# Differential attention heads: one weighted sum of a difference instead of two, with new step lists for the last layer

## The chip, the core and the metric

The kernel runs on one core of a Trainium2 chip. The metric is the device time of one execution in microseconds (us), the median of the runs. Five engines of the core work side by side and meet at semaphores: TensorE (PE; its weight loads are shown apart as PEld), VectorE (DVE), ScalarE (ACT), GpSimd (POOL) and the DMA queue of SyncE (SP). TensorE writes to PSUM alone; its operands come from SBUF.

## What is computed

A token matrix x of 256 x 1024 (float32) goes through four layers: two of one model and two of another. The change touches the fourth, `odd_layer`. Its core, cut to what matters:

```python
cq, ckv, kpe, qd, kd, vd, gate = _split(rmsnorm(x) @ w_in, SPLIT_O)
q  = (rmsnorm(cq) @ w_cq_b)                    # 8 latent heads of 96
kv = (rmsnorm(ckv) @ w_ckv_b)                  # 8 heads: 64 of key, 64 of value
oc = attend_blocks(qc, kc, v_c, 96 ** -0.5)    # 8 latent heads
# 4 differential heads, each with two queries and two keys of 64, one value of 128:
s1 = einsum('bqhd,bkhd->bhqk', q1, k1) * scale
s2 = einsum('bqhd,bkhd->bhqk', q2, k2) * scale
p  = softmax(s1) - lam * softmax(s2)
od = einsum('bhqk,bkhd->bqhd', p, v)
od = rmsnorm(od, g_sub_d) * (1.0 - lam_init)
x  = x + (concat([oc, od]) * silu(gate)) @ w_out
```

`lam` is one scalar, worked out from four small vectors.

## The kernel before

Every projection is a product in three passes: a weight tile and the activations are split into a high part (ACT, L853, `hi`) and a low part (DVE, L1288, `lo`), and PE multiplies high x low, high x high and low x high (L2053 to L2055; the gate's columns at L2130 to L2133). Weights stream through a ring of 8 slots of 128 x 1024; each slot is a **unit** (chunk, number). In the fourth layer chunks 0 to 5 are the projections, 6 and 7 the gate, 8 and 9 the output projection.

Attention is cut into instances of one softmax over 256 x 256, numbered j = 2p + h (pair p, half h). Pairs 0 to 3 are the four differential heads, their two halves being the two softmaxes. Pairs 4 to 7 hold two latent heads each. The steps, with the engine on which each stands:

- `prep k` (PE, L2032) transposes queries and keys, `D k` (ACT or DVE) copies them out of PSUM. prep 0 to 3 are differential, prep 4 to 11 latent heads. Before them stand, on DVE, `RED` (sums of squares), `SCL` (scaling), `GN` (gains), `ROT` (rotation) and `KCAT`, with `SQ` on ACT and `POW` (a power of 16 values, L755) on POOL, for qd, kd (differential) and qc, kc (latent).
- `S p` (PE, L2227) scores of both halves; `X p,h` (DVE, L1437) row maximum; `E p,h` (ACT, L985 and L987) exponential, with the row sum.
- `SC p,h` (DVE, L1594 to L1609) multiplies the exponentials by a factor per row: the reciprocal of the row sum, and in half 1 of a differential pair also by `lam[:, 2:3]`, which holds the negative of lambda (L1606).
- `T p,h` (PE, L2264) transposes the weights into one of two PSUM banks, `C p,h` (ACT, L997) copies them to `probT`.
- `PV p` (PE, L2249) adds up the value products of the pair. For a differential pair both halves add into the same 128 rows of PSUM, so the subtraction happens there.
- `OD` (ACT, L954 and L955) takes the result of a differential pair out. Its normalisation is a chain: `ODSUM` (PE, L2531), `ODMS` (DVE, L1982), `ODP` (POOL, L831), `DG` (DVE, eight instructions, L1987), `OF` (PE, L2539), and `ON` (DVE, L1994), which also needs `ODG` (POOL, L835), the product with the gate. `SILU` (ACT) makes the gate ready.
- `MP`, `MH`, `ML` (DVE, ACT, DVE) split a latent pair's result; `out 0,k` is unit (8,k). `take c` (ACT and DVE) copies a projection's chunk out of PSUM, and `gt` one of the gate.

What sets the order: four lists, `PE_3`, `ACT_3`, `DVE_3` and `POOL_3`, one per engine, each carried out strictly in turn. The PSUM bank for transposed data alternates in the order in which prep and T steps stand in `PE_3` (`FILL`). Weights, DMAs and the other three layers have lists of their own.

Of the kernel before, what the change touches and what calls it, by code (L numbers as in the profile page):

```python
# [8 lines left out]
ALU = mybir.AluOpType  # L9
# [5 lines left out]
T = 256  # L15
NT = T // P
D = 1024
# [115 lines left out]
FILL = {}  # L133
# [139 lines left out]
for _kind, *_at in PE_2:  # L273
    if _kind == "prep":
        number("prep2", _at)
    elif _kind == "T":
        number("attn2", (2 * _at[0] + _at[1],))
PE_3 = [("unit", 1, 0), ("unit", 1, 1), ("unit", 1, 2), ("unit", 1, 3), ("unit", 2, 0), ("F", 0), ("unit", 2, 1),
        ("unit", 2, 2), ("unit", 2, 3), ("F", 1), ("unit", 3, 0), ("unit", 3, 1), ("prep", 0), ("prep", 1),
        ("unit", 4, 0), ("prep", 2), ("unit", 5, 0), ("S", 0), ("unit", 5, 1), ("unit", 5, 2), ("S", 1),  # L280
        ("unit", 5, 3), ("prep", 3), ("T", 0, 0), ("unit", 6, 0), ("unit", 6, 1), ("S", 2), ("T", 0, 1),
# [3 lines left out]
        ("unit", 7, 3), ("prep", 10), ("T", 4, 1), ("ODSUM",), ("prep", 7), ("prep", 11), ("S", 6), ("T", 5, 0),  # L285
        ("PV", 4), ("OF",), ("T", 5, 1), ("S", 7), ("PV", 5), ("out", 0, 0), ("T", 6, 0), ("T", 6, 1), ("out", 0, 1),
        ("T", 7, 0), ("T", 7, 1), ("PV", 6), ("PV", 7), ("out", 0, 2), ("out", 0, 3)]

ACT_3 = [("take", 0), ("LAMX",), ("hi", 2, 0), ("hi", 2, 1), ("hi", 2, 2), ("hi", 2, 3), ("hi", 3, 0), ("hi", 3, 1),
# [11 lines left out]

DVE_3 = [("take", 0), ("LAMD",), ("GT",), ("LS",), ("lo", 2, 0), ("lo", 2, 1), ("lo", 2, 2), ("lo", 2, 3),
         ("lo", 3, 0), ("LAMS",), ("LSC",), ("take", 1), ("lo", 3, 1), ("lo", 4, 0), ("RED", "qd"), ("LL", 0),
         ("lo", 5, 0), ("lo", 5, 1), ("SCL", "qd"), ("take", 2), ("ROT", "qd"), ("RED", "kd"), ("lo", 5, 2),
         ("LL", 1), ("take", 3), ("SCL", "kd"), ("ROT", "kd"), ("take", 4), ("KCAT",), ("RED", "qc"), ("lo", 5, 3),
# [10 lines left out]

POOL_3 = [("POW", "lora"), ("POW", "qd"), ("POW", "kd"), ("POW", "qc"), ("POW", "kc"), ("ODP",), ("ODG",)]


number("norm6", range(4))  # L320
# [32 lines left out]
def net(nc, a, out):  # L353
# [37 lines left out]
    fac = place("fac", [P, 72, 2])  # L391
# [12 lines left out]
    prob = place("prob", [P, 4, 512])  # L404
# [13 lines left out]
    OF = (SUM, 2)  # L418
# [15 lines left out]
    kd = extra[:, 0:2560].rearrange("p (t h c d) -> p t h c d", t=NT, h=10, c=2)  # L434
# [31 lines left out]
    lam = small[:, 296:300]  # L466
# [104 lines left out]
    def instances(stage):  # L571
        out = []
# [25 lines left out]
        if stage == "attn3":  # L598
            for h in range(8):
                out.append(dict(q=pair_row("prep3", "qd", h), k=pair_row("prep3", "kd", h), bias=None,  # L600
                                v=(z3, 1440 + P * (h // 2), P), causal=False, half=0, pair=h // 2,
                                first=h % 2 == 0, last=h % 2 == 1, lam=h % 2 == 1))
            for h in range(8):
                out.append(dict(q=reg[0:MLA_D, BLOCK["prep3"]["qc", h], :], k=reg[0:MLA_D, BLOCK["prep3"]["kc", h], :],
                                bias=None, v=(lo_kv, P * h + HD, HD), causal=False, half=h % 2, pair=4 + h // 2,
                                first=True, last=True))
# [91 lines left out]
    def heads_of(name):  # L698

        return {"qd": heads(z3[:, :, 416:928]), "kd": heads(z3[:, :, 928:1440]), "qc": heads(lo_q, MLA_D), "kc": kcat}[name]  # L700

    def product_of(stage, p):

# [136 lines left out]
    def _(act):  # L840
# [136 lines left out]
        def exponents(stage, j):  # L977

            i, it = INST0[stage] + j, INST[stage][j]
            act.wait_ge(max_ready, i + 1)  # L980
            if it["bias"] is None and j >= 4:
                act.wait_ge(t_filled, FILL[stage, j - 4] + 1)
            w = P if it["causal"] else T
            src, sign = (ps[:, score_bank(i), :], 1.0) if it["bias"] is None else (prob[:, i % 4, :], -1.0)
            n.activation(prob[:, i % 4, 0:w], src[:, 0:w], ACT.Exp, bias=negm[:, i, 0:1], scale=sign,  # L985
                         accum_out=den[:, i, 0:1])
            n.activation(prob[:, i % 4, 256:512], src[:, 256:512], ACT.Exp, bias=negm[:, i, 1:2], scale=sign,  # L987
                         accum_out=den[:, i, 1:2]).then_inc(exp_ready, 1)
# [277 lines left out]
    def _(dve):  # L1266
# [4 lines left out]
        def link(ins):  # L1271

            chain[0] += 1
            ins.then_inc(sem("dve_chain"), 1)
            dve.wait_ge(sem("dve_chain"), chain[0])
# [324 lines left out]
        def scaled(stage, p, h):  # L1600

            if h == 0:
                factors(stage, p)
            k = INST0[stage] + 2 * p + h
            if INST[stage][2 * p + h].get("lam"):
                link(v.tensor_tensor(fac[:, k, :], fac[:, k, :], bc(lam[:, 2:3], [P, 2]), ALU.mult))  # L1606
            w = P if INST[stage][2 * p]["causal"] else T
            v.tensor_scalar(prob[:, k % 4, 0:w], prob[:, k % 4, 0:w], fac[:, k, 0:1], None, ALU.mult)
            v.tensor_scalar(prob[:, k % 4, 256:512], prob[:, k % 4, 256:512], fac[:, k, 1:2], None, ALU.mult)\  # L1609
             .then_inc(probs_ready, 1)  # L1610
# [402 lines left out]
    def _(pe):  # L2013
# [217 lines left out]
        def weighted(stage, j0):  # L2231
# [3 lines left out]
            for j in two:  # L2235
                it, p = inst[j], inst_pair(stage, j)
                if it["opens"] and p >= 2:
                    pe.wait_ge(*bank_taken(p - 2))
            for j in two:
                f = FILL[stage, j]  # L2240
                pe.wait_ge(t_drained[f % 2], f // 2 + 1)
            for kt in range(NT):
                for j in two:
                    i, it, p = i0 + j, inst[j], inst_pair(stage, j)
                    buf, lo, w = it["v"]
                    rows = slice(64 * it["half"], 64 * it["half"] + w)
# [3 lines left out]
                                   start=it["first"] and kt == 0, stop=it["last"] and kt == NT - 1,  # L2250
                                   skip_group_check=True)
                    if kt == NT - 1:
                        ins.then_inc(pv_done, 1)

        def transposed(stage, j):

# [390 lines left out]
```

## Time and profile before

| | |
|---|---|
| median of 3 runs | 919.93 us (919.16 to 924.9) |
| the profiled execution | 921.26 us, of which the span is 919.4 us |
| PE busy | 882.9 us, 96% of the span |
| DVE, ACT, POOL busy | 624.9, 493.8, 79.0 us |
| DMA | 148.71 MB, 162 GB/s mean |
| the fourth layer's step lists | from about 778 us to 905 us |

The 1.86 us between the profiled execution's time and its span lie outside all engines' work. Matmul rows of a timeline overlap by the pipeline, so the cost of a piece on PE is the distance between starts, not the duration of a row.

### The profile page before, as it was taken

The numbers are of one execution on the slowest core, as the hardware profiler recorded it, in microseconds if no ns is written. First come the engines' busy times: TensorE is split into PE (matmuls) and PEld (weight loads), VectorE is DVE, ScalarE is ACT, GpSimd is POOL, SyncE is SP. The second block draws the span as 40 slices with busy tenths as digits, with TensorE's granted clock in tenths as the row PEclk, the third lists the DMA queues.
The fourth block names the chain that finished last, engine by engine and source line by source line (L and its number), as shares of the span: only waits on it lengthen the run. The fifth ranks groups of instructions, "written<-read, shape, count | busy, mean of one in ns | idle before, by whom it ended". The sixth has DMA issues, their size and how long they took to land.

```text
span 919.4 us, 14636 instructions
## 1 busy us (share of the span) xinstructions
PE 882.9 (96%) x5540; PEld 755.7 (82%) x5540; DVE 624.9 (68%) x1139; ACT 493.8 (54%) x913; POOL 79.0 (9%) x88
## 2 busy tenths in 40 slices
PE   4999899999999999999999999998999999989998
PEld 3868578999998878777899999886879868868976
DVE  4788987455564467877655555545588777989873
ACT  4446865454553345666544444434456775565662
POOL 2100000000000000000000000000386000231010
PEclk9999999999999999999999999998999999999999
DMA  9664135655566556433655555664854314745201
GB/s 340 206 209 151 37 98 178 184 184 183 184 224 187 184 172 194 152 124 115 192 162 179 185 183 189 228 190 143 251 166 144 128 38 131 218 136 147 84 24 46
DMA packets 96789, 148.71 MB, mean 162 GB/s; under 512 B 6272, under 2 KB 59680, under 8 KB 96592
## 3 DMA queue, kind: packets, MB, share of 16 engines
q1 hardware_dynamic: 94512, 140.50, 48.6%
q10 hardware_dynamic: 1296, 4.87, 1.6%
q0 software_dynamic: 912, 2.41, 1.0%
q8 instruction: 45, 0.74, 0.3%
q14 instruction: 24, 0.20, 0.1%
HBM read 146.71 MB, written 1.05 MB: 161 GB/s over the span
## 4 chain that ended last, share of the span: by engine, by line
PE 79%; issue 6%; DVE 6%; POOL 4%; ACT 3%; DMA 2%; SPq 0%; POOLq 0%; DVEq 0%; ACTq 0%
PE ps L2053 22%; PE ps L2055 22%; PE ps L2054 21%; PE ps L2227 3%; PE ps L2249 3%; PE ps L2264 2%; POOL small L755 1%; PE ps L2043 1%; DVE w_lo L1288 1%; ACT hA L868 1%; PE ps L2032 1%; DMA w_raw<-in_w_in_e 1%; POOL extra L797 1%; PE ps L2130 1%; PE ps L2133 1%
## 5 line engine op out<-in xcount | busy, mean ns | idle before, releaser
L1288 DVE TENSOR_TENSOR w_lo<-w_raw,w_hi 128x1024 fp32r<-128x1024 f32 (+1 forms) x261 | 310.1, 1207 | 132.5 <-ACT w_hi L853 128.4
L853 ACT ACTIVATE w_hi<-w_raw 128x1024 fp32r<-128x1024 f32 (+1 forms) x261 | 267.2, 1041 | 156.4 <-DMA w_raw<-in_w_gate_up 56.4
L2053 PE MATMUL ps<-w_hi,hT_lo 128*128 128x512 f32 (+3 forms) x448 | 176.9, 395 | 6.6 <-DVE w_lo L1288 4.7
L2053 PE MATMUL ps<-hT_hi,w_lo 128*128 128x256 f32 x640 | 181.4, 283 | 0.0
L2055 PE MATMUL ps<-hT_lo,w_hi 128*128 128x256 f32 x640 | 181.1, 283 | 0.0
L2054 PE MATMUL ps<-hT_hi,w_hi 128*128 128x256 f32 x640 | 181.1, 283 | 0.0
L2055 PE MATMUL ps<-w_lo,hT_hi 128*128 128x512 f32 (+3 forms) x448 | 171.5, 383 | 0.0
L2054 PE MATMUL ps<-w_hi,hT_hi 128*128 128x512 f32 (+3 forms) x448 | 171.4, 383 | 0.0
L2053 PEld LDWEIGHTS ps<-hT_hi,w_lo 128*128 128x128 f32 x640 | 122.9, 192 | 0.4 <-DVE w_lo L1288 0.3
L2054 PEld LDWEIGHTS ps<-hT_hi,w_hi 128*128 128x128 f32 x640 | 122.9, 192 | 0.0
L2055 PEld LDWEIGHTS ps<-hT_lo,w_hi 128*128 128x128 f32 x640 | 122.9, 192 | 0.0
L2053 PEld LDWEIGHTS ps<-w_hi,hT_lo 128*128 128x128 f32 x448 | 85.7, 191 | 29.0 <-issue 7.8
L2055 PEld LDWEIGHTS ps<-w_lo,hT_hi 128*128 128x128 f32 x448 | 85.6, 191 | 16.3
L2054 PEld LDWEIGHTS ps<-w_hi,hT_hi 128*128 128x128 f32 x448 | 85.9, 192 | 14.1
L2053 PE MATMUL ps<-w_hi,hid_lo 128*128 128x512 f32 x176 | 69.5, 395 | 0.0
L2055 PE MATMUL ps<-w_lo,hid_hi 128*128 128x512 f32 x176 | 69.4, 395 | 0.0
L2054 PE MATMUL ps<-w_hi,hid_hi 128*128 128x512 f32 x176 | 69.4, 394 | 0.0
L997 ACT ACTIVATE probT<-ps 128x384 f32<-128x384 f32 (+1 forms) x72 | 37.5, 539 | 31.6 <-PE ps L2264 28.8
L760 POOL TENSOR_TENSOR small<-small 128x1 f32<-128x1 f32 x10 | 5.6, 556 | 482.6 <-DVE small L1295 482.6
L2227 PE MATMUL ps<-reg 64*128 64x256 f32 (+2 forms) x288 | 39.8, 371 | 2.4 <-ACT prob L987 2.2
L2264 PE MATMUL ps<-table,prob 128*128 128x128 f32 x248 | 38.5, 279 | 1.4 <-DVE prob L1609 0.6
L2053 PEld LDWEIGHTS ps<-w_hi,hid_lo 128*128 128x128 f32 x176 | 33.2, 188 | 7.6
(235 smaller groups left out, 1196.8 us busy)
## 6 DMA issues: line engine op xcount, KB each, us to landing
w_raw<-in_w_gate_up SPq DMA_DIRECT2D x176, 256.0 KB, 4.3
w_raw<-in_w_down SPq DMA_DIRECT2D x44, 512.0 KB, 4.3
w_raw<-in_w_in_e SPq DMA_DIRECT2D x38, 512.0 KB, 5.2
w_raw<-in_w_qkv_o SPq DMA_DIRECT2D x24, 512.0 KB, 4.4
w_raw<-in_w_in_o SPq DMA_DIRECT2D x20, 512.0 KB, 3.7
w_raw<-in_w_out_e SPq DMA_DIRECT2D x16, 512.0 KB, 3.5
w_raw<-in_w_out_o SPq DMA_DIRECT2D x16, 512.0 KB, 3.5
w_raw<-in_w_in_e SPq DMA_DIRECT2D x8, 268.0 KB, 4.9
```

The lines of the kernel that those rows point to most:

```text
L755: g.tensor_tensor(o, i, halfs[:, 0:n], ALU.pow).then_inc(sem(name + "_rstd"), 1)
L797: pool.dma_start(bias_na[64 * half:64 * half + 64, :, u, :], src).then_inc(sem("bias_in"), 16)
L853: n.activation(w_hi[:, u % RING, 0:size], w_raw[:, u % RING, 0:size], ACT.Copy).then_inc(hi_ready, 1)
L868: n.activation(hA[:, t, cols], x[:, t, cols], ACT.Square, scale=D ** -0.5, accum_out=ss[:, 2 * t + c:2 * t + c + 1]).then_inc(norm_sem("ss ...
L997: n.activation(probT[:, i % 4, 0:w], ps[:, TB + f % 2, 0:w], ACT.Copy).then_inc(t_drained[f % 2], 1)
L1288: v.tensor_tensor(w_lo[:, u % RING, 0:size], w_raw[:, u % RING, 0:size], w_hi[:, u % RING, 0:size].bitcast(F32), ALU.subtract).then_inc(lo ...
L2053: m.matmul(o, lhs[1], rhs[0], start=start, stop=False)
L2054: m.matmul(o, lhs[0], rhs[0], start=False, stop=False)
L2055: return m.matmul(o, lhs[0], rhs[1], start=False, stop=stop)
L2227: ins = m.matmul(o, it["q"][:, t * P:(t + 1) * P], it["k"][:, 0:w], start=True, stop=True)
L2249: ins = m.matmul(ps[rows, OB + p % 2, cols], buf[:, kt, lo:lo + w], probT[:, i % 4, src], start=it["first"] and kt == 0, stop=it["last"] a ...
L2264: ins = m.transpose(ps[:, TB + f % 2, col:col + P], prob[:, i % 4, 256 * t + kt * P:256 * t + kt * P + P], ident)
```

## The change

The instances of the differential heads get a mark `diff`, and each is now its own sum (`first` and `last` both true). In `SC p,1` of such a pair the two multiplications by the factor give way to two SCALAR_TENSOR_TENSOR instructions: half 1 times its factor, plus the already scaled half 0, in place. Then `T p,1` alone is done (`T p,0` and `C p,0` are gone for p < 4), and `PV p` multiplies that one matrix with the values: two matmuls in the program instead of four. The exponentials of pair p + 2 wait for `T p,1` also where they waited for `T p,0`. All four lists of the fourth layer are replaced.

```diff
-        ("unit", 2, 2), ("unit", 2, 3), ("F", 1), ("unit", 3, 0), ("unit", 3, 1), ("prep", 0), ("prep", 1),
-        ("unit", 4, 0), ("prep", 2), ("unit", 5, 0), ("S", 0), ("unit", 5, 1), ("unit", 5, 2), ("S", 1),
...
+        ("unit", 2, 2), ("unit", 2, 3), ("F", 1), ("unit", 3, 0), ("unit", 3, 1), ("prep", 1), ("unit", 4, 0),
+        ("prep", 0), ("unit", 5, 0), ("prep", 2), ("unit", 5, 1), ("prep", 3), ("S", 0), ("unit", 5, 2),
+        ("unit", 5, 3), ("S", 1), ("T", 0, 1), ("unit", 6, 0), ("PV", 0), ("unit", 6, 1), ("S", 2), ("unit", 6, 2),
...
-                                first=h % 2 == 0, last=h % 2 == 1, lam=h % 2 == 1))
+                                first=True, last=True, lam=h % 2 == 1, diff=True))
...
+    def turned(stage, j):
+
+        return j | 1 if INST[stage][j].get("diff") else j
...
-                act.wait_ge(t_filled, FILL[stage, j - 4] + 1)
+                act.wait_ge(t_filled, FILL[stage, turned(stage, j - 4)] + 1)
...
+            if h and INST[stage][2 * p].get("diff"):
+                dve.wait_ge(probs_ready, k)
+                for t in range(NT):
+                    row = slice(T * t, T * t + T)
+                    ins = v.scalar_tensor_tensor(out=prob[:, k % 4, row], in0=prob[:, k % 4, row],
+                                                 scalar=fac[:, k, t:t + 1], in1=prob[:, (k - 1) % 4, row],
+                                                 op0=ALU.mult, op1=ALU.add)
+                ins.then_inc(probs_ready, 1)
+                return
...
-            for j in two:
+            used = tuple(j for j in two if turned(stage, j) == j)
+            for j in used:
                 f = FILL[stage, j]
                 pe.wait_ge(t_drained[f % 2], f // 2 + 1)
             for kt in range(NT):
-                for j in two:
+                for j in used:
...
-                        ins.then_inc(pv_done, 1)
+                        ins.then_inc(pv_done, 2 // len(used))
```

The first place where the lists put work elsewhere and the prediction speaks of it is PE around the end of the differential heads' normalisation (`ps` is PSUM, `table` the identity or, in the rows L2531 and L2539, the squares and diagonals). PE before, from prep 7 to PV 5:

```order
L2032 MATMUL ps<-table,hA 96x128 x4
L2264 MATMUL ps<-table,prob 128x128 x4
L2531 MATMUL ps<-table 128x1 x8
L2032 MATMUL ps<-table,extra 96x128 x4
L2032 MATMUL ps<-table,hA 96x128 x4
L2227 MATMUL ps<-reg 128x256 x4
L2264 MATMUL ps<-table,prob 128x128 x4
L2249 MATMUL ps<-probT,extra 64x256 x4
L2539 MATMUL ps<-table 128x512 x2
L2264 MATMUL ps<-table,prob 128x128 x4
L2227 MATMUL ps<-reg 128x256 x4
L2249 MATMUL ps<-probT,extra 64x256 x4
```

The same place now (line numbers of the new file):

```order
L2044 MATMUL ps<-table,extra 96x128 x4
L2044 MATMUL ps<-table,hA 96x128 x4
L2544 MATMUL ps<-table 128x1 x8
L2239 MATMUL ps<-reg 128x256 x4
L2277 MATMUL ps<-table,prob 128x128 x8
L2262 MATMUL ps<-probT,extra 64x256 x4
L2552 MATMUL ps<-table 128x512 x2
L2277 MATMUL ps<-table,prob 128x128 x8
L2262 MATMUL ps<-probT,extra 64x256 x4
```

Between ODSUM (128x1) and OF (128x512) stood two preps, S 6, T 5,0 and PV 4; now S 7, T 5,0, T 5,1 and PV 4 stand there.

The second place is DVE between `KCAT` and the first `SC 0,1`. Now, from the end of KCAT (`small` holds the sums, `negm` the maxima, `fac` the factors):

```order
L1291 TENSOR_TENSOR w_lo<-w_raw,w_hi 128x1024 x2
L1748 TENSOR_REDUCE small<-reg 128x16
L1750 TENSOR_SCALAR small<-small 128x16
L1440 TENSOR_REDUCE negm<-ps 128x2 x2
L1756 TENSOR_TENSOR hA<-hA,small 128x2x768
L1597 RECIPROCAL fac<-den 128x4
L1620 TENSOR_SCALAR prob<-prob,fac 128x256
L1621 TENSOR_SCALAR prob<-prob,fac 128x256
L1945 COPY reg<-ps 128x512
L1609 TENSOR_TENSOR fac<-fac,small 128x2
L1614 SCALAR_TENSOR_TENSOR prob<-prob,fac 128x256 x2
```

The rows L1748 and L1750 come twice in turn there (RED kc, then RED qc; shown once). Before, one RED stood ahead of X 0,0 and X 0,1, and no SCL between them and SC 0,0; now two REDs and SCL kc (the row L1756) do.

## Rows read from the trace of the kernel before

**Rows 1.** PE's waits in 797:919.4: engine, line waited for, us in total, times, longest.
```profile
PE ps L2032 <- DVEq L1926: 2.7, 1, 2.7
PE ps L2539 <- DVE table L1987: 1.7, 1, 1.7
PE ps L2032 <- DVE lr_lo L1956: 0.6, 1, 0.6
```
**Rows 2.** Windows: busy PE, PEld, DVE, ACT, POOL; granted clock; DMA share, GB/s.
```profile
820.00:822.00 2.00, 2.00 (x6) 1.58 (x5) 1.85 (x2) 0.00 (x0) 0.00 (x0) 0.50 0.00 0
```
**Rows 3.** PE's timeline at PV 1: start, duration, line, tiles, matmuls.
```profile
848.07 0.60 PE L2264 MATMUL ps<-table,prob 128*128 128x128 f32 x4
848.51 1.89 PE L2249 MATMUL ps<-probT,z 128*128 128x256 f32 x8
850.33 1.14 PE L2227 MATMUL ps<-reg 64*128 64x256 f32 x8
```
**Rows 4.** PE's timeline, 808:824: matmuls of one shape at either clock.
```profile
820.46 0.63 PE L2053 MATMUL ps<-w_hi,hT_lo 128*128 128x512 f32 x1
820.89 0.63 PE L2054 MATMUL ps<-w_hi,hT_hi 128*128 128x512 f32 x1
...
822.17 0.40 PE L2054 MATMUL ps<-w_hi,hT_hi 128*128 128x512 f32 x1
822.40 0.40 PE L2055 MATMUL ps<-w_lo,hT_hi 128*128 128x512 f32 x1
```
**Rows 5.** DVE's timeline: a scaling, then a two-input instruction of the same length.
```profile
844.00 0.35 DVE L1609 TENSOR_SCALAR prob<-prob,fac 128x256 f32<-128x256 f32 x1
...
846.06 0.42 DVE L1380 TENSOR_TENSOR tmp<-extra,table 128x256 f32<-128x256 f32 x1
```
**Rows 6.** DVE's timeline: SCL kd, RED qc, a split, D 1, SCL qc; ODMS.
```profile
813.69 1.23 DVE L1744 TENSOR_TENSOR z<-z,small 128x1024 f32<-128x1024 f32 x1 [1.26 <-POOL small L755]
...
820.40 1.75 DVE L1736 TENSOR_REDUCE small<-reg 128x16 f32<-128x1536 f32 x1
...
825.10 1.22 DVE L1288 TENSOR_TENSOR w_lo<-w_raw,w_hi 128x1024 fp32r<-128x1024 f32 x1
826.23 0.69 DVE L1933 COPY reg<-ps 128x512 f32<-128x512 f32 x1
...
828.29 1.75 DVE L1744 TENSOR_TENSOR extra<-extra,small 128x1536 f32<-128x1536 f32 x1
...
878.94 0.17 DVE L1982 TENSOR_SCALAR small<-ps 128x8 f32<-128x8 f32 x1 [2.11 <-PE ps L2531]
```
**Rows 7.** POOL's timeline: two powers of 16 values, and ODG (L835).
```profile
799.16 2.91 POOL L755 TENSOR_TENSOR small<-small 128x16 f32<-128x16 f32 x1 [9.33 <-DVE small L1738]
...
822.45 3.94 POOL L755 TENSOR_TENSOR small<-small 128x16 f32<-128x16 f32 x1 [8.79 <-DVE small L1738]
...
881.00 2.40 POOL L835 TENSOR_TENSOR z<-z 128x1024 f32<-128x1024 f32 x1
```
**Rows 8.** The chain that ended last, at DG: start, us, what.
```profile
880.89 2.19 DVE table L1987 x2
...
883.40 1.25 DVE table L1987 x6
```
**Rows 9.** PE's timeline: scores of latent heads, and ODSUM.
```profile
861.52 1.89 PE L2227 MATMUL ps<-reg 96*128 96x256 f32 x8
...
876.98 1.92 PE L2531 MATMUL ps<-table 128*128 128x1 f32 x16
```
**Rows 10.** PE's timeline after two earlier idle times.
```profile
637.04 1.70 PE L2043 MATMUL ps<-table,hA 128*128 128x128 f32 x8 [2.46 <-DVE hA L1305]
...
640.38 0.63 PE L2054 MATMUL ps<-w_hi,hT_hi 128*128 128x512 f32 x1
...
738.30 1.13 PE L2227 MATMUL ps<-reg 64*128 64x256 f32 x8 [2.24 <-ACT prob L987]
```
**Rows 11.** Windows again: the stretch around 738.
```profile
720.00:760.00 40.00, 37.34 (x259) 28.80 (x258) 29.86 (x69) 30.80 (x75) 0.00 (x0) 1.00 0.25 77
```

More of the change, by code:

```diff
@@ L278 @@
 PE_3 = [("unit", 1, 0), ("unit", 1, 1), ("unit", 1, 2), ("unit", 1, 3), ("unit", 2, 0), ("F", 0), ("unit", 2, 1),
-        ("unit", 2, 2), ("unit", 2, 3), ("F", 1), ("unit", 3, 0), ("unit", 3, 1), ("prep", 0), ("prep", 1),
-        ("unit", 4, 0), ("prep", 2), ("unit", 5, 0), ("S", 0), ("unit", 5, 1), ("unit", 5, 2), ("S", 1),
-        ("unit", 5, 3), ("prep", 3), ("T", 0, 0), ("unit", 6, 0), ("unit", 6, 1), ("S", 2), ("T", 0, 1),
[3 rows of a table removed]
[L285 to L289, printed above, removed]
[11 rows of a table removed]
[L302 to L305, printed above, removed]
[10 rows of a table removed]
-POOL_3 = [("POW", "lora"), ("POW", "qd"), ("POW", "kd"), ("POW", "qc"), ("POW", "kc"), ("ODP",), ("ODG",)]
+        ("unit", 2, 2), ("unit", 2, 3), ("F", 1), ("unit", 3, 0), ("unit", 3, 1), ("prep", 1), ("unit", 4, 0),
+        ("prep", 0), ("unit", 5, 0), ("prep", 2), ("unit", 5, 1), ("prep", 3), ("S", 0), ("unit", 5, 2),
+        ("unit", 5, 3), ("S", 1), ("T", 0, 1), ("unit", 6, 0), ("PV", 0), ("unit", 6, 1), ("S", 2), ("unit", 6, 2),
+        ("prep", 6), ("unit", 6, 3), ("prep", 4), ("S", 3), ("T", 1, 1), ("prep", 5), ("unit", 7, 0), ("prep", 8),
[4 rows of a table added]
+        ("out", 0, 3)]
+ACT_3 = [("take", 0), ("hi", 2, 0), ("LAMX",), ("hi", 2, 1), ("hi", 2, 2), ("hi", 2, 3), ("hi", 3, 0), ("hi", 3, 1),
[10 rows of a table added]
+DVE_3 = [("GT",), ("take", 0), ("LAMD",), ("lo", 2, 0), ("LS",), ("lo", 2, 1), ("lo", 2, 2), ("LSC",), ("lo", 2, 3),
[13 rows of a table added]
+POOL_3 = [("POW", "lora"), ("POW", "qd"), ("POW", "kd"), ("POW", "kc"), ("POW", "qc"), ("ODP",), ("ODG",)]
 number("norm6", range(4))
```

51 rows, old and new, of tables (ACT_3, DVE_3, PE_3) are left out of this document.

## Prediction

> **What bounds the kernel now.** I read the page first: in the small table above PE is busy for 96% of the span, so matmuls removed count unless PE then waits. The table of PE's waits in the fourth layer comes next [rows 1]: only three are named, 0.64, 2.75 and 1.71 us. They are the opening of prep 1's PSUM bank (DVE had yet to take LL 1, the low part of F 1), prep 2's wait for the rotated keys kd, and OF's wait for DG. Then the windows: behind the 2.75 us the granted clock is 0.50 of full speed, that is 1.2 instead of 2.4 GHz [rows 2], and a matmul of 512 columns starts every 0.43 us instead of every 0.23 [rows 4]. Eight of them ran so, from 818.75 to 822.17: 8 x 0.2 = 1.6 us. What PE lost in this layer is thus 0.64 + 2.75 + 1.6 + 1.71 = **6.7 us**. The timelines of DVE, ACT and POOL are read last, for whether they can keep up: what a step of PE waits for is a date on one of them.
>
> **What goes.** On PE, per differential head, one T and half of PV. T costs 0.44 us and PV 1.82, from start to start [rows 3]. Four heads: 4 x 0.44 + 4 x 0.91 = **5.4 us**, all on an engine with nothing beside it. The matmul records of PV are eight for four instructions, and halve to four. ACT loses four C of 0.5 us each; ACT has idle time before most exponentials, so I cost that at nothing.
>
> **What is added.** DVE: in SC p,1 two TENSOR_SCALAR of 0.35 us become SCALAR_TENSOR_TENSOR with two inputs; no row shows these operands. The nearest is a TENSOR_TENSOR of equal length, 0.42 us [rows 5]. So 8 x 0.07 = 0.6 us over the layer. Below, it could be nothing (0.35); above, a row of twice the length would be 0.7, or 8 x 0.35 = 2.8 us in all. I take 0.42, since length and inputs agree. The Trainium skill speaks against the change here ("VectorE: DVE Perf Modes", Mode 2x_2P): a float32 tensor_scalar may use both read ports for one tensor and make two results a cycle, which an instruction with two tensors can't. By its rate the difference would be an estimated 256 / 0.96 GHz / 2 = 0.13 us each, 1.1 us in all, and by it T 0,1 would come 0.1 us later and the gain be 5.8. The wait for the own earlier SC p,0 is met, since the factor's product stands between.
>
> **Where PE waits now.** I followed the new lists with the durations of before, noting at each step of PE when its producers finish.
>
> 1. Unit 4,0 now follows prep 1, and still needs LL 1 at 811.5: 0.7 us, as before.
> 2. Prep 2 was late because ROT kd was. Between now stand prep 0 and unit 5,0 (2.8 us). But ROT kd moves too: D 1 (0.6) is put ahead of SCL kd, where POOL's power was late anyway (813.69 [rows 6]), so it is hidden; take 4 (1.2) is put ahead of ROT kd, so kd is ready at 818.95 and not 817.7. PE stands at prep 2 at about 818.3. Small waits at the second half of unit 5,0 (DVE's take 4), at prep 2 and at S 0 (D 2, behind SQ kc and a split on ACT) come to 0.4 + 0.7 + 0.4 = 1.5 us, each under a microsecond, and no fall of the clock.
> 3. **T 0,1** is the new late one. DVE before did SCL kd, ROT kd, take 4, KCAT and a first RED from 813.69 to 822.4 (820.40, 1.75 and the small instruction behind it, 2.0 in all [rows 6]). The same five stand there now with two splits among them, each 1.13 from start to start (825.10 to 826.23): RED kc ends at 824.5 to 824.7. POOL then takes 2.9 to 3.9 us for the power [rows 7]; DVE does RED qc (2.0) and both X (1.2) meanwhile, to 827.7. SCL kc takes 1.8, like SCL qc at 828.29 [rows 6]; a drain and the two SC of a pair took 826.23 to 828.29, 2.1 us, and now 0.2 more: SC 0,1 is done at 831.8 to 832.5. PE has S 0 at 823.15, then two units, S 1, and stands at T 0,1 at 831.0. Wait 0.8 to 1.5; I take 1.2. Units 5,2 and 5,3, S 1 and the steps behind have no other cover.
> 4. Up to unit 7,0 DVE runs nearly without a pause; its split for unit 6,3 is ready 0.1 us before it is used and that for 7,0 0.4 us late. 0.4 us.
> 5. **OF.** Count from the end of unit 7,3. DG ends after prep 7 and 11 (0.9), ODSUM (1.8), then ODMS to DG, 878.94 to 880.89 (1.95: POOL's ODP lies between), then DG itself, 880.89 to 884.65 (3.76 [rows 6, 8]): 8.4 us. PE is there after 0.9 + 1.8 + S 7 1.7 + two T 0.8 + PV 4 1.0 = 6.2 us (ODSUM and S by [rows 9] less 0.1 to 0.2 of overlap, prep and T by [rows 3], and a latent PV, whose values are 64 wide, near half of a differential one). Wait **2.2 us**. So OF waits longer than before, though ODSUM now stands later in front of more latent work.
> 6. Behind OF nothing is late: SC 7,0 is done some 0.5 us before T 7,0, ML 7 more than 1 us before out 0,3.
>
> Waits now: 0.7 + 1.5 + 1.2 + 0.4 + 2.2 = **6.0 us**, but no slow clock. The sum is 5.4 + 6.7 - 6.0 = 6.1; a few more switches between kinds of matmuls (0.2) leave **5.9 us**. Against the profiled execution: span 919.4 - 5.9 = 913.5 and time 921.26 - 5.9 = 915.4. That execution was 1.3 us over the median, so the median should be 919.93 - 5.9 = **914.0 us**.
>
> **Why DG is slow, and one rival.** Two of DG's eight instructions take 2.19 us, the other six 1.25 [rows 8], and the first two lie exactly under ODG on POOL, 881.00 to 883.40 [rows 7]. This is what the Trainium skill says ("SBUF — State Buffer", Who interferes with whom): DVE in a 2-port mode and GpSimd exclude each other for a whole instruction. Now SILU, and with it ODG's permission, ends 4.7 us after unit 7,3 by my count, and ODP also at 4.7; DG is free at 4.8. They meet again. If SILU comes over 1.6 us later, DG runs in 8 x 0.21 = 1.7 us and OF waits 0.1 us: gain 5.9 + 2.1 = 8.0, 911.9 us. Chance 14%. With luck at T 0,1 and unit 7,0 as well it passes 9.2.
>
> **The other ways.**
> - The clock falls behind OF's wait. After idle times of 2.24 us it stayed at 1.00 [rows 10, 11]; after 2.46, with a further pause, a matmul took 0.63 us and not 0.40 [rows 10, 4]; here it is 2.2. Cost 1.6 us, as measured in [rows 4]: 915.6 us. Chance 22%.
> - DVE binds longer. From T 0,1 to unit 7,0 the margins are 0.1 to 0.8 us, so each us by which DVE falls behind is PE's. Against it stands that no DVE row there is new but the SC. With 2 to 3 us more: 916.5 us. Chance 13%.
> - POOL's powers block the two-input instructions. By the lock rule cited above a scaling or split with two inputs would stand still during a power. SCL kc and SC 0,1 would lie under the power for qc, up to 3.94 us [rows 7]. The trace speaks against it: the split at 825.10 takes its usual 1.22 us [rows 6] inside the power of 822.45 to 826.39. Should it hold: 5.9 - 3.9 = 2.0 gain, 917.9 us. Chance 3%.
> - Slower than before: the clock falls three times, around 815 to 819, at T 0,1 and at OF. Price 3 x 1.6 = 4.8 us; if each low stretch is 3 matmuls longer, as the one after 639.8 was (11), 3 x 2.2 = 6.6, which is more than the gain: 920.6 us. It decides where the waits of a few steps join to over 2.4 us. Chance 2%; a loss over 1% needs more still.
> - The change doesn't shorten PE, because PV's cost is not its matmuls but the switch. Against it speak the eight matmul records in 1.82 us, evenly 0.23 apart like those of a projection [rows 3, 4]. Gain then 5.9 - 3.6 = 2.3: 917.6 us. Chance 2%.
>
> The forecast itself has 44%, with 4.7 to 7.4 us of gain (the bounds of T 0,1's and OF's waits, each +-0.4, and of the SC) for its own range. The **range** takes in the falling clock, a freed DG and some of a binding DVE: 910.0 to 918.0 us. About 1% of the time, 9.2 us, is what a measurement of this kernel can tell from no change. More than that needs nearly every wait gone (5.4 + 6.7 is all there is): 9%. Slower by as much 2%, within 1% 89%.
>
> **What the new profile would show.** L2277 on PE in the fourth layer with 12 T instead of 16, PV of a differential head at 0.9 us; the SCALAR_TENSOR_TENSOR near 0.42 us; no 2.75 us wait and granted clock near 1.00 in 815 to 824; a wait of about 1 us at T 0,1 for DVE, of about 2 us at OF for DG, with ODG over DG's first two instructions; and the last chunk ending some 6 us earlier. Wrong would be: a DVE that is later than counted at several steps (my times are sums of some twenty durations), a slow clock behind either wait, or SILU later than DG.

## The result, and the profile after

The changed kernel takes 915.13 us (median of 7 runs, 913.99 to 916.63) where the kernel before, run beside it on the same chip, takes 920.72 (7 runs): a ratio of 0.9939, 95% interval 0.9927 to 0.9952, or 5.6 us less. Timed a second time beside others it was 914.71 against 919.81 us: 0.9945 [0.9932, 0.9957], 5.1 us. (The prediction took 9.2 us as the least that can be told from no change; the interval here is some 1.2 us to either side, so the gain is clear of it.) The profiled execution fell from 921.26 to 915.67 us, and its span from 919.4 to 913.9.

The page of the changed kernel, its first lines: span, then busy time and share of each engine.

```profile
span 913.9 us, 14571 instructions
PE 879.2 (96%) x5508; PEld 751.1 (82%) x5508; DVE 625.8 (68%) x1139; ACT 491.5 (54%) x909; POOL 77.2 (8%) x88
```

PE's share is unchanged, as it must be when removed work and lost waits are both a few us of 900. The views that answer the prediction are those of the fourth layer. First the table of PE's waits, 790 to the end (engine, line waited for, us in total, times, longest), which stands against [rows 1]; then the first two lines of the same table of the second profile of the same kernel, which is run e9 below.

```profile
PE ps L2277 <- DVE prob L1614: 0.8, 1, 0.8
PE ps L2065 <- ACT extra L1196: 0.8, 2, 0.5
PE ps L2552 <- DVE table L1999: 0.6, 1, 0.6
PE ps L2239 <- ACT reg L1215: 0.4, 1, 0.4
PE ps L2142 <- DVE w_lo L1291: 0.3, 1, 0.3
PE ps L2044 <- DVEq L1938: 0.3, 1, 0.3
```
```profile
PE ps L2552 <- DVE table L1999: 2.2, 1, 2.2
PE ps L2277 <- DVE prob L1614: 0.8, 1, 0.8
```

The wait of 2.75 us at prep 2 is 0.3 now. In its place stand six small ones, T 0,1's wait for SC 0,1 (L1614) the largest, and OF's wait for DG, which is 0.6 us in one execution and 2.2 in the other. PE's timeline of the two around OF (start, duration, line, tiles, matmuls, idle time before and its releaser) says why. The first execution:

```profile
873.76 1.92 PE L2544 MATMUL ps<-table 128*128 128x1 f32 x16
875.54 2.06 PE L2239 MATMUL ps<-reg 96*128 96x256 f32 x8
877.39 1.92 PE L2277 MATMUL ps<-table,prob 128*128 128x128 f32 x8
879.24 1.79 PE L2262 MATMUL ps<-probT,extra 128*64 128x256 f32 x8
881.58 1.98 PE L2552 MATMUL ps<-table 128*128 128x512 f32 x4 [0.55 <-DVE table L1999]
```

The second execution of the same kernel:

```profile
873.58 1.92 PE L2544 MATMUL ps<-table 128*128 128x1 f32 x16
875.36 1.97 PE L2239 MATMUL ps<-reg 96*128 96x256 f32 x8
877.17 1.04 PE L2277 MATMUL ps<-table,prob 128*128 128x128 f32 x8
878.14 1.08 PE L2262 MATMUL ps<-probT,extra 128*64 128x256 f32 x8
881.39 1.99 PE L2552 MATMUL ps<-table 128*128 128x512 f32 x4 [2.17 <-DVE table L1999]
```

In the first, T 5,0, T 5,1 and PV 4 take 1.92 and 1.79 us and not 1.04 and 1.08, and OF waits 1.6 us less for it. Its windows (columns as in [rows 2]) show the cause, a granted clock of 0.50:

```profile
876.00:878.00 2.00, 2.00 (x11) 1.73 (x10) 0.73 (x3) 1.64 (x1) 1.92 (x2) 0.82 0.01 3
878.00:880.00 2.00, 2.00 (x11) 1.43 (x11) 2.00 (x1) 1.24 (x3) 2.00 (x1) 0.50 0.00 0
880.00:882.00 2.00, 1.45 (x7) 0.53 (x4) 2.00 (x9) 1.24 (x1) 0.07 (x1) 0.82 0.00 0
```

The slow clock lay in front of a wait that ended by DVE's date, so it cost nothing: OF starts at 881.58 and 881.39 in the two, 32.3 us before the end in both. Two more pairs among the experiments below agree: e1 without a fall and e12 with one in this place are equally long in this stage (109.6 us), and so are, within 0.1 us, e11 without and e2 with one.

**Where the time went, by kinds of work.** Timelines of PE were added up from the transposes of F 1 (the same place in every list) to the end of the span, each row counted from its start to the start of the next and named idle time set apart. "Waits" is that idle time. Us:

| kernel | F 1 at | to the end | T, PV | units | preps, F 1 | S, ODSUM, OF | waits | clock low at |
|---|---|---|---|---|---|---|---|---|
| before | 805.8 | 113.6 | 18.5 | 69.6 | 5.6 | 14.8 | 5.1 | 818 to 822 |
| changed, first | 806.0 | 107.9 | 14.7 | 68.4 | 6.7 | 14.9 | 3.3 | 877 to 881 |
| changed, second | 805.8 | 107.9 | 13.1 | 68.4 | 6.7 | 14.8 | 4.9 | - |

From the kernel before to the changed one's second profile: T and PV -5.5, units -1.2 (the slow clock, 1.6, lay on them: so +0.4), preps +1.1, waits -0.2; together 5.7 with rounding. DVE's new instruction, before the wait at T 0,1, and DG with POOL's ODG beside it, in the first execution:

```profile
827.88 1.75 DVE L1756 TENSOR_TENSOR hA<-hA,small 128x1536 f32<-128x1536 f32 x1
...
829.88 0.35 DVE L1620 TENSOR_SCALAR prob<-prob,fac 128x256 f32<-128x256 f32 x1
830.15 0.35 DVE L1621 TENSOR_SCALAR prob<-prob,fac 128x256 f32<-128x256 f32 x1
...
831.19 0.88 DVE L1614 SCALAR_TENSOR_TENSOR prob<-prob,fac 128x256 f32<-128x256 f32 x2
831.99 0.68 DVE L1350 COPY z<-ps 128x512 f32<-128x512 f32 x1
...
877.67 3.85 DVE L1999 TENSOR_SCALAR table<-table,small 128x128 f32<-128x128 f32 x8 [1.27 <-POOL small L834]
```
```profile
827.59 2.96 POOL L758 TENSOR_TENSOR small<-small 128x16 f32<-128x16 f32 x1
...
875.96 1.68 POOL L834 TENSOR_TENSOR small<-small 128x8 f32<-128x8 f32 x1 [45.42 <-DVE small L1994]
877.72 2.35 POOL L838 TENSOR_TENSOR z<-z 128x1024 f32<-128x1024 f32 x1
```

The step that T 0,1 waits for ends at 832.07; SCL kc, the two instructions of SC 0,0 and the two of SC 0,1 stand there. ODG again lies on DG's first part, and DG takes 3.85 us.

### The profile page after: what moved, and what is told of

The parts are those of the page before. It is cut to its first block, busy times and chain, and to the rows that moved or that the text cites. A ratio compares the mean times of both kernels' runs of the same rounds, so it can differ in the third digit from the quotient of the medians.

```text
span 913.9 us, 14571 instructions
## 1 busy us (share of the span) xinstructions
PE 879.2 (96%) x5508; PEld 751.1 (82%) x5508; DVE 625.8 (68%) x1139; ACT 491.5 (54%) x909; POOL 77.2 (8%) x88
## 3 DMA queue, kind: packets, MB, share of 16 engines
HBM read 146.71 MB, written 1.05 MB: 162 GB/s over the span
## 4 chain that ended last, share of the span: by engine, by line
PE 81%; DVE 8%; POOL 3%; issue 3%; ACT 2%; DMA 2%; SPq 0%; POOLq 0%; DVEq 0%; ACTq 0%
PE ps L2065 22%; PE ps L2067 21%; PE ps L2066 21%; PE ps L2239 3%; PE ps L2262 3%; PE ps L2277 3%; DVE w_lo L1291 2%; PE ps L2142 1%; PE ps L2055 1%; PE ps L2145 1%; PE ps L2144 1%; PE ps L2044 1%; ACT hA L871 1%; POOL small L758 1%; DMA w_raw<-in_w_in_e 1%
## 5 line engine op out<-in xcount | busy, mean ns | idle before, releaser
L1000 ACT ACTIVATE probT<-ps 128x384 f32<-128x384 f32 (+1 forms) x68 | 35.3, 534 | 25.9 <-PE ps L2277 23.0
L2067 PEld LDWEIGHTS ps<-w_lo,hid_hi 128*128 128x128 f32 x176 | 33.2, 188 | 7.7
L2066 PEld LDWEIGHTS ps<-w_hi,hid_hi 128*128 128x128 f32 x176 | 33.2, 188 | 7.7
```

Source lines behind the costliest of these rows:

```text
L1000: n.activation(probT[:, i % 4, 0:w], ps[:, TB + f % 2, 0:w], ACT.Copy).then_inc(t_drained[f % 2], 1)
L2066: m.matmul(o, lhs[0], rhs[0], start=False, stop=False)
L2067: return m.matmul(o, lhs[0], rhs[1], start=False, stop=stop)
```

## The experiments

Twelve runs were made, of eight new kernels (four of the runs repeat a kernel), in three groups (e1 to e4, e5 to e8, e9 to e12), each group on one chip with the kernel before beside it: 920.08, 921.34 and 919.81 us. Medians of different groups do not compare; the ratios do, and only the last group has the changed kernel in it. "To the end" is the length from F 1 as above and "waits" the named waits in it, both in the profiled execution; the last column is where the clock was low in the fourth layer.

| experiment | median, us | ratio to before, 95% | to the end | waits | clock low at |
|---|---|---|---|---|---|
| e1 new math, old lists | 916.94 | 0.9969 [0.9957, 0.9981] | 109.6 | 7.1 | - |
| e2 old math, new lists | 920.5 | 0.9998 [0.9989, 1.0007] | 112.2 | 2.6 | 878 to 882 |
| e3 changed, ODG held | 914.51 | 0.9932 [0.9920, 0.9944] | 107.3 | 2.8 | 876 to 880 |
| e4 before, ODG held | 918.82 | 0.9983 [0.9970, 0.9997] | 110.4 | 3.8 | - |
| e5 changed, SCL kc later | 916.05 | 0.9941 [0.9929, 0.9954] | 108.7 | 5.4 | - |
| e6 changed, D 3 on ACT | 916.85 | 0.9947 [0.9927, 0.9968] | 108.9 | 4.4 | 882 to 886 |
| e7 e3 and e6 together | 914.24 | 0.9925 [0.9909, 0.9941] | 105.3 | 2.3 | - |
| e8 e7, ODSUM earlier | 914.85 | 0.9928 [0.9915, 0.9941] | 108.2 | 3.4 | 875 to 879 |
| e9 changed again | 914.71 | 0.9945 [0.9932, 0.9957] | 107.9 | 4.9 | - |
| e10 e7 again | 911.7 | 0.9923 [0.9909, 0.9936] | 105.3 | 2.3 | - |
| e11 e2 again | 919.75 | 1.0005 [0.9995, 1.0014] | 112.3 | 4.3 | - |
| e12 e1 again | 917.75 | 0.9971 [0.9958, 0.9983] | 109.6 | 5.3 | 875 to 879 |

**The two halves of the change (e1, e2, and again e12, e11).** e1 and e12: the changed kernel's code with the lists of before, less the steps that no longer exist.

```diff
-        ("unit", 5, 3), ("prep", 3), ("T", 0, 0), ("unit", 6, 0), ("unit", 6, 1), ("S", 2), ("T", 0, 1),
+        ("unit", 5, 3), ("prep", 3), ("unit", 6, 0), ("unit", 6, 1), ("S", 2), ("T", 0, 1),
...
```

> The new computation of the differential heads with the old lists, from which only T p,0 and C p,0 of the four differential pairs are struck. Theory (the gain is the 5.4 us of TensorE work removed, and the lists only keep it): TensorE reaches T 2,1 some 3 us earlier than before while VectorE's SC 2,1 is not earlier, so about 1.4 us are given back there; the wait of OF stays near 1.7 and prep 2's 2.75 with its slow clock too. Gain 4.0 us against the kernel before, between 3.5 and 5.0. Rival (the searched lists earn the gain, the removed matmuls alone turn into waits for VectorE): gain under 2 us.

> The new computation in the old order of work. Theory: 2.5 to 3.5 us faster than before (ratio 0.9962 to 0.9973), as in its first comparison, and so with the lists alone at 1 to 2.5 the two parts add up to the change's 5 to 6. Rival: 4.5 to 5.4 us (0.9941 to 0.9951), all of TensorE's removed work.

e2 and e11: the code of before with the changed lists, and the steps it needs put in.

```diff
-        ("unit", 5, 3), ("S", 1), ("T", 0, 1), ("unit", 6, 0), ("PV", 0), ("unit", 6, 1), ("S", 2), ("unit", 6, 2),
+        ("unit", 5, 3), ("S", 1), ("T", 0, 0), ("T", 0, 1), ("unit", 6, 0), ("PV", 0), ("unit", 6, 1), ("S", 2), ("unit", 6, 2),
...
```

> The old computation with the new lists, T p,0 and C p,0 put directly ahead of T p,1 and C p,1. Theory: the lists save 6.7 us of waits and slow clock and bring 4 to 6 us of new waits, of which T 0,0 takes 0.4 us under its cover; against the kernel before 0.3 to 1.5 us faster. Rival (the lists earn most of it): 3 us faster or more. Rival (they suit only the shorter work): slower than before.

> The kernel before with the new order of work and the old computation. Its profile had 2.4 us less of waits and slow clock from 811 us on than that of before, its median no gain at all. Theory: the lists alone are worth 1 to 2.5 us (ratio 0.9973 to 0.9989), and the first comparison lost them in clock falls elsewhere. Rival: nothing again (0.9990 to 1.0007): the lists pay only with the new computation.

Measured: the new math alone brings 0.9969 and 0.9971, some 2.8 us, and not 4.0; the new lists alone bring nothing, twice. Together they bring 5.1 to 5.6. So the halves do not add: some 2.5 us come only with both. Each of these figures has an interval of about 1 us to either side; the lengths of the stage, which repeat to 0.1 us, say the same with a share of 1.8 us: 112.1 before where the clock doesn't fall (worked out from e4 below), 109.6 with the math alone, 112.2 and 112.3 with the lists alone, 107.9 with both. PE's waits in e12 and e11 (columns as above) show what each half lacks. New math, old lists:

```profile
PE ps L2045 <- DVEq L1939: 3.5, 2, 2.7
PE ps L2045 <- DVE lr_lo L1969: 0.6, 1, 0.6
PE ps L2143 <- ACT z L1197: 0.4, 1, 0.4
PE ps L2545 <- DVE z L1991: 0.3, 1, 0.3
PE ps L2278 <- ACT probT L1001: 0.2, 1, 0.2
PE ps L2143 <- DVE w_lo L1292: 0.2, 1, 0.2
```

New lists, old math:

```profile
PE ps L2538 <- DVE table L1986: 2.2, 1, 2.2
PE ps L2052 <- ACT extra L1192: 0.8, 2, 0.5
PE ps L2031 <- ACT probT L996: 0.6, 1, 0.6
PE ps L2226 <- ACT reg L1211: 0.4, 1, 0.4
PE ps L2031 <- DVEq L1925: 0.3, 1, 0.3
```

With the old lists the 2.7 us at prep 2 stay, and PE, 5 us shorter, runs into five more that [rows 1] did not have (2.0 us: 0.77 of the first line, and the last four lines). With the new lists and the old math, that wait goes but OF's grows to 2.2, and the preps and F 1 cost 6.2 us and not 5.6. Neither forecast of e1 held by the median: 2.8 us (interval 1.7 to 4.0) lies between the theory's 3.5 to 5.0 and the rival's 2. The new waits are there, but none of them is at T 2,1, where the theory had put 1.4 us. The expectation of e12 came true. The expectation of e11, that the lists are worth 1 us or more, fell; of e2's 0.3 to 1.5 us the interval of e11 leaves at most 0.5.

**ODG held until DG is done (e3, e4).** In e3 on the changed kernel and in e4 on the kernel before, GpSimd gets one more wait ahead of the gate product ODG; all else stays.

```diff
+                pool.wait_ge(sem("od_diag"), 1)
```

> The changed kernel, with GpSimd's product with the gate (ODG) waiting until VectorE's eight DG instructions are done. Theory (the two exclude each other): DG takes 8 x 0.2 = 1.7 us and not 3.85, OF's wait of 0.55 us is gone, and gain over the changed kernel is 0.5 us where TensorE's clock is still at half speed on the way there, up to 1.6 us where it is not. ON 0 finds ODG done. Rival (DG is slow by itself): eight rows of 0.48 us, no gain, and up to 1 us lost at ON 0.

> The same wait of ODG for DG in the kernel before. Theory: DG from 880.9 to 882.6 instead of 884.65, TensorE gets to OF at 883.0 and no longer waits 1.71 us: 1.7 us faster than before, ratio 0.998. Rival (DG is slow by itself, or ODG being later holds ON up): same time or slower.

DG takes 1.66 us in both, and not 3.85 or 3.76, so it is not slow by itself. e4 is 1.6 us faster than before by the ratio, as expected: OF's 1.71 us are gone. e3 came out at 0.9932, 0.7 us below the changed kernel in the ratio, inside both intervals. Its profile shows why no more: OF's wait is gone, but the clock is low from 876 to 880 in it, and without the wait nothing covers that. To the end it is 107.3: 107.9 - 2.2 + 1.6.

**What binds at T 0,1 (e5, e6).** e5 moves SCL kc out of SC 0,1's way; e6 gives D 3 to ACT. First e5, in DVE's list:

```diff
-         ("RED", "kc"), ("RED", "qc"), ("X", 0, 0), ("X", 0, 1), ("SCL", "kc"), ("SC", 0, 0), ("D", 3), ("SC", 0, 1),
-         ("take", 5), ("X", 1, 0), ("lo", 6, 1), ("SCL", "qc"), ("X", 1, 1), ("GN", "qc"), ("lo", 6, 2),
+         ("RED", "kc"), ("RED", "qc"), ("X", 0, 0), ("X", 0, 1), ("D", 3), ("SC", 0, 0), ("SC", 0, 1),
+         ("take", 5), ("SCL", "kc"), ("X", 1, 0), ("lo", 6, 1), ("SCL", "qc"), ("X", 1, 1), ("GN", "qc"), ("lo", 6, 2),
```

In e6 D 3 also leaves DVE's list, where it stood between SC 0,0 and SC 0,1; ACT's list becomes

```diff
-         ("SQ", "kc"), ("hi", 6, 1), ("D", 2), ("E", 0, 0), ("E", 0, 1), ("hi", 6, 2), ("take", 5), ("C", 0, 1),
+         ("SQ", "kc"), ("hi", 6, 1), ("D", 2), ("D", 3), ("E", 0, 0), ("E", 0, 1), ("hi", 6, 2), ("take", 5), ("C", 0, 1),
```

> The changed kernel with one edit in VectorE's list: SCL kc (1.75 us) moves from ahead of SC 0,0 to behind take 5, D 3 goes ahead of SC 0,0. My theory: VectorE has no pause from 820 to 850 us in the changed kernel, so it is what sets TensorE's pace there; T 0,1's wait (0.84 us) goes, but take 5 and the lo steps keep their dates, the unit before unit 7,0 and unit 7,0 wait instead, and the end stays: within 0.3 us of the changed kernel (ratio to the kernel before 0.993 to 0.995). Rival: the wait at T 0,1 is a matter of order alone and is gained whole, 0.8 us (ratio about 0.993 or below), and no wait of over 0.4 us appears between 832 and 850.

> The changed kernel with one edit: D 3, the drain of prep 3 (0.6 us), leaves VectorE for ScalarE, behind D 2. If VectorE's amount of work binds between 820 and 850 us, the wait at T 0,1 falls from 0.84 to about 0.2 us, unit 7,0's 0.35 goes, and the whole is 0.6 to 1.0 us faster than the changed kernel (ratio to before about 0.993). Rival: ScalarE, which then exponentiates and takes operands later, gives the wait back before unit 6,2 or at prep 6 (the same time as the changed kernel, a wait of 0.4 or more on ScalarE between 832 and 850).

e5: The ratio, 0.9941, is where the theory had it. T 0,1 waits no more, and PE waits in units instead. The waits of 832 to 850 in it:

```profile
PE ps L2142 <- DVE w_lo L1291: 1.6, 3, 0.7
PE ps L2239 <- ACT prob L990: 0.2, 1, 0.2
```

The third of the L2142 waits, 0.34 at 849.9, was there in the changed kernel; 0.52, 0.72 and the 0.17 on ACT are new, 1.4 us for 0.85. So the order alone gains nothing there, which is what an engine bound by its amount of work would show; e6, which takes work away, tests it: T 0,1's wait falls to 0.25 as expected; the 0.34 before unit 7,0 does not go, a miss. The gain of 0.6 to 1.0 us does not show either; its ratio, 0.9947, cannot be told from the changed kernel's. In the profile OF waits 2.19 us and then the clock falls. Windows, and OF:

```profile
882.00:884.00 2.00, 1.95 (x3) 0.92 (x4) 1.52 (x3) 1.37 (x7) 0.00 (x0) 0.57 0.00 0
884.00:886.00 2.00, 2.00 (x6) 0.86 (x6) 1.68 (x5) 0.56 (x4) 0.00 (x0) 0.58 0.00 0
```
```profile
882.05 3.61 PE L2552 MATMUL ps<-table 128*128 128x512 f32 x4 [2.19 <-DVE table L1999]
```

That is the first of the prediction's other ways, with its price: 3.61 - 1.98 = 1.6 us.

**Both edits (e7, again e10), and the place of ODSUM (e8).** e7 is e3 and e6 in one. e8 is e7 with

```diff
-        ("prep", 11), ("ODSUM",), ("S", 7), ("T", 5, 0), ("T", 5, 1), ("PV", 4), ("OF",), ("T", 6, 0), ("T", 6, 1),
+        ("ODSUM",), ("prep", 11), ("S", 7), ("T", 5, 0), ("T", 5, 1), ("PV", 4), ("OF",), ("T", 6, 0), ("T", 6, 1),
```

> Both single edits that ought to help on the changed kernel: D 3 on ScalarE, and ODG (the product of the gate with silu on GpSimd) held until DG is done. If they act at different places and so add: 0.6 to 1.0 us from the first and 0.7 from the second, 1.3 to 1.7 us faster than the changed kernel, ratio to the kernel before 0.9920 to 0.9930. Rival: what the first brings is lost between 850 and 877 us, where TensorE would meet operands, and only 0.7 stays (0.9932).

> D 3 on ScalarE and ODG held until DG is done, on the changed kernel, beside the changed kernel on the same chip. Counted from unit 5,0's start to the end and without slow clock, the profiles give 95.7 us for it and 98.4 less 1.7 = 96.7 for the changed kernel. Theory: 1.0 to 2.0 us faster than the changed kernel (ratio to before 0.9915 to 0.9930). Rival: the two are the same within 0.5 us, since the wait before OF and the slow clock take each other's place.

> The kernel with D 3 on ScalarE and the held gate product, and one edit in TensorE's list: ODSUM (16 matmuls of one column) goes between prep 7 and prep 11, where it stood behind both and directly ahead of S 7. It tells what the granted clock follows. Theory: the clock falls to 0.50 behind ODSUM wherever TensorE goes from ODSUM into S 7, T 5,0 and T 5,1; with prep 11 between them the fall goes or halves. The price is a wait of 0.3 us at ODSUM on OD 3 and 0.4 at S 7 on D 11; without the fall 1.6 us of slow clock come back, so 0.5 to 1.0 us faster than with the two edits alone. Rival A: the fall comes all the same (rows at 0.50 behind S 7), and the kernel is 0.3 to 0.7 us slower. Rival B: the fall isn't in every execution, so the time moves by less than 0.4 us whatever the profile shows.

e7 and e10, one kernel, are the fastest: 0.9925 [0.9909, 0.9941] and 0.9923 [0.9909, 0.9936]. Expected of e7 was 0.9920 to 0.9930. The kernel beats the one before clearly; its interval and that of the changed kernel in the same group (0.9932 to 0.9957) just overlap. In the last group, on one chip, it is 3.0 us under the changed kernel by medians (911.7 and 914.71) and 2.0 by the two ratios; 1.0 to 2.0 was expected. Both profiles have 105.3 us to the end, 2.6 less than the changed kernel: 2.17 at OF and 0.6 at T 0,1, less 0.17 that is new at T 6,0. Both profiled executions are the fastest of their groups (910.07 where the median of e7 is 914.24) and have no low clock in this layer, so 2.6 us is what the stage gains without one. GpSimd, DVE and PE in e10:

```profile
872.59 1.67 POOL L834 TENSOR_TENSOR small<-small 128x8 f32<-128x8 f32 x1 [44.81 <-DVE small L1995]
876.14 2.35 POOL L839 TENSOR_TENSOR z<-z 128x1024 f32<-128x1024 f32 x1 [1.87 <-DVE table L2000]
```
```profile
874.30 1.66 DVE L2000 TENSOR_SCALAR table<-table,small 128x128 f32<-128x128 f32 x8 [1.26 <-POOL small L834]
```
```profile
876.02 1.98 PE L2553 MATMUL ps<-table 128*128 128x512 f32 x4
```

DG takes 1.66 us instead of 3.85, and OF has no idle time ahead of it.

e8 was meant to tell what the clock follows, and its profile fits rival A: waits of 0.45 at ODSUM and 0.83 ahead of S 7, and a granted clock of 0.50 from 876 to 878. But its ratio is 0.0003 from e7's, 0.3 us, which is within the noise and fits rival B as well, and e7 and e10 had no low clock with ODSUM directly ahead of S 7. The theory fell: the place of ODSUM alone is not what decides.

**The changed kernel once more (e9).**

> The changed kernel itself, beside the three others of this call on one chip. The profiles so far show that the granted clock falls to 0.50 at about the same places (636 to 646, 734 to 744, and one in the fourth layer) in some executions and not in others, so kernels timed in different calls can differ by 1 to 2 us for that alone. Theory: 5.0 to 6.0 us faster than before (ratio 0.9935 to 0.9945). Rival: the first comparison was favourable, and it is 3.5 to 4.5.

5.1 us, as the theory had it.

## Why the prediction was right

Forecast was 914.0 us and 5.9 us of gain; measured were 915.1 and 914.7, with 5.6 and 5.1. The main terms (what goes, where PE waits, DG beside ODG) were right; that the sum came so close is in part luck, as the terms below show. Most of the way to the 915.1 is the chip's: before was 920.7 in that comparison and not 919.9. By the steps of the prediction:

- **What goes, 5.4 us.** Right: T and PV fell by 5.5 us. PV of a differential head takes 0.87 us from start to start (853.33 to 854.20), 0.91 was taken.
- **SC.** Undersized. I took durations, 0.42 for 0.35. From start to start it is 0.40 (831.19 to 831.99 for two) against 0.27 (829.88 to 830.15): 0.13 us each, 1.1 us on DVE and not 0.6. That is the estimate by the rate which the Trainium skill states ("VectorE: DVE Perf Modes", Mode 2x_2P), and the trace agrees with it. By this count it moved T 0,1 by 0.1 us.
- **Waits, 6.0 us.** Measured 4.9 (e9): 0.47 at unit 4,0 for 0.7, and for take 3 on ACT, not for LL 1; 0.34 at unit 5,0, 0.32 at prep 2 and 0.42 at S 0 for 1.5 (the first at the unit's start, for take 4 on ACT, not at its second half for DVE); 0.85 at T 0,1 for 1.2; 0.35 at unit 7,0 for 0.4; 2.17 at OF for 2.2. All at the units and steps named; the early ones 0.6 too high.
- **Switches, 0.2 us.** The step that failed. Preps and F 1 cost 1.1 us more and the units 0.4: 1.5 us. Of the single preps one took 0.59 us before and the others 0.39 to 0.44; now five take 0.53 to 0.60, and the pairs take 1.05 and 1.14 us, not 0.79 and 0.89. A part of this is not a price of switching. A row of four transposes lasts 0.60 us, and the next step starts under its last 0.14 to 0.25 us unless it has to wait; the idle time that the profile names is counted from the row's end. Before, prep 11 with S 6 behind it, and now prep 0 with the wait of unit 5,0 (e9):

```profile
879.22 0.60 PE L2032 MATMUL ps<-table,hA 128*96 128x128 f32 x4
879.65 1.89 PE L2227 MATMUL ps<-reg 96*128 96x256 f32 x8
```
```profile
814.41 0.60 PE L2044 MATMUL ps<-table,z 128*128 128x128 f32 x4
815.35 0.47 PE L2065 MATMUL ps<-w_hi,hT_lo 128*128 128x512 f32 x1 [0.34 <-ACT extra L1196]
```

  The first switches to scores and takes 0.43 us; the second takes its 0.60 and then waits. The one prep of 0.59 before stands directly ahead of a named wait, and so do four of the five now (ahead of unit 4,0, unit 5,0, S 0 and unit 7,0); in e12, with the old lists, the three preps ahead of new named waits take 0.60 to 0.61 too. A named wait thus costs some 0.17 us more than its number, by the step ahead of it: with three more behind preps than before, an estimated 0.5 of the 1.1 us. For the rest (0.53 ahead of S 3, the pairs ahead of S 4 and ODSUM, rows in the units) no wait is named, and the rows do not part switches from waits too short to be named. The waits were forecast 1.1 too high and the switches 1.3 too low, so the two errors nearly cancelled, and a good third of the second is waiting under another name: 5.4 + 6.7 - 6.0 - 0.2 = 5.9 was forecast, 5.5 + 6.7 - 4.9 - 1.5 = 5.8 is what the rows give, for a stage that is 5.7 shorter.
- **The slow clock of before, 1.6 us.** Counted as gained in every execution, from one profile. e4, whose order of PE is that of before, waits 2.74 us at prep 2 too and has a clock of 1.00 behind it, and so have e1 and e12 with 2.74 and 2.73:

```profile
818.00:820.00 2.00, 1.24 (x8) 1.12 (x9) 1.82 (x4) 2.00 (x3) 0.00 (x0) 1.00 0.55 207
820.00:822.00 2.00, 2.00 (x10) 1.45 (x8) 1.75 (x4) 0.26 (x1) 0.00 (x0) 1.00 0.00 0
```

  Without it the stage of before is 110.4 + 1.7 = 112.1 us and the gain 4.2. Of the unprofiled runs only the mean clock is on record, not where it fell; the measured gains, 5.1 and 5.6, lie between 4.2 and 5.7. So this term is right for the execution that was profiled; one of four profiles with this wait has the fall, so on average it is probably too high.
- **The clock behind OF's wait.** It did not fall there in the changed kernel's two profiles, but did in e6, at the price named. The reason given, no fall after 2.24 us of idle time and one after 2.46, does not hold: none followed 2.73 and 2.74 us at prep 2, and one followed 2.19 in e6.
- **OF and DG.** Right in place, size and mechanism: SILU ended at 877.64, DG began at 877.67, and ODG met it. e3, e4 and e10 show that the meeting is what makes DG long. The Trainium skill ("SBUF — State Buffer", Who interferes with whom) has VectorE in a 2-port mode and GpSimd exclude each other, and these runs agree. The rival of a freed DG was priced at 2.1 us; e10's OF gives 2.17.
- **POOL's powers.** The trace shows that they block nothing: inside the power from 827.59 to 830.55, SCL kc took its 1.75 us and two TENSOR_SCALAR 0.35 each. It had 3%.
- **DVE binds longer.** DVE's work does set PE's pace from 820 to 850 (e5, and T 0,1's wait in e6), but it was not later than counted: SC 0,1 ended at 832.07 for 831.8 to 832.5. That rival costs nothing here and 0.8 us in e5.
- **No loss.** The clock did fall in the new order: ahead of OF, where it was free, and in e6 behind OF, where it cost 1.6 us. In this layer it never fell more than once. (The forecast gives 2% both to slower at all and to slower by 1%; a loss of over 1% had to get less.)

## What to carry to other kernels

Count the waits of a new order, and not only their length: each costs the overlap with the step ahead of it too, 0.17 us here, which no table of waits shows. Seven waits, as in the changed kernel, make 1.2 us of it by this estimate, more than the whole wait at T 0,1. Where removed work meets waits for other engines, the two parts of an edit need not add; run each alone, and expect a part of the gain to come only when the order is fitted to the new load. And set apart a term that one profile shows by chance (a clock that fell) from one that every execution has, for instance by the length of the changed stage in two profiles: it agreed to 0.1 us for each of the four kernels that were profiled twice, where whole runs differed by 2.

## What the runs showed of the hardware

The granted clock falls to 0.50 in some executions of a program and not in others, at about the same places. Of the fourteen profiles (before, changed, twelve experiments) twelve have it low within 634 to 646 us (e11 has it at 668 to 672 instead, e7 not at all) and nine within 734 to 744; in the fourth layer seven have it. All run the same code up to the fourth layer, and F 1 stands anywhere from 802.7 to 807.1 us; that is wider than most gains here. Windows of the second profile of the changed kernel; that of before has 1.00 from 734 to 744:

```profile
736.00:738.00 2.00, 1.23 (x9) 0.86 (x10) 1.19 (x5) 2.00 (x8) 0.00 (x0) 0.93 0.00 0
738.00:740.00 2.00, 2.00 (x10) 1.67 (x12) 2.00 (x5) 1.64 (x7) 0.00 (x0) 0.50 0.00 0
```
Of the five profiles without a low clock at 734 to 744, four have one in the fourth layer; of the nine with it, three. That is too few to call it a rule, and no experiment took it apart. Nor need PE have been idle by much: ahead of 877 in the changed kernel it had no named wait from 850 on. An OF wait of 2.2 us was followed by a low clock in e6 and not in e9, e11 or e5 (2.09). What decides is open. What it costs is known: 1.6 us where PE's own work sets the pace (OF in e6, 3.61 for 1.98), nothing where a longer wait for another engine comes behind it (OF of the changed kernel).
